# Attention in a hybrid diffusion block: a pair's products with the values split over two rounds, and the scaled maximum moved from ScalarE to GpSimd

## The chip, the cores and the metric

One Trainium2 chip, and of it one core. The metric is the device time of one execution of the whole program in microseconds (us), a median over runs. TensorE (PE, with its weight loads shown as PEld), VectorE (DVE), ScalarE (ACT), GpSimd (POOL) and SyncE (SP) each run their own instruction stream in order, and meet only at semaphores.

## What is computed

A two-layer backbone over 512 latent and 256 context tokens of width 1024. Layer 0 mixes tokens with grouped-query attention, layer 1 with a long convolution; both are followed by an MLP. The change touches only the attention of layer 0, for the latent queries:

```python
def gqa_attend(q, k, v):
    s = jnp.einsum('bqkgd,bskd->bkgqs', q, k).astype(jnp.float32) * (q.shape[-1] ** -0.5)
    p = jax.nn.softmax(s, axis=-1).astype(v.dtype)
    return jnp.einsum('bkgqs,bskd->bqkgd', p, v)
```

There are 8 query heads of width 128 over 2 key/value heads, 512 queries and 768 keys. The queries and keys are RMS-normed before; the kernel leaves the query's root out of the scores and applies it as the factor `rq`, one number per query row and tile.

## The kernel before

The work is written by hand, one stream per engine, with a semaphore for each kind of result. A value in full precision is held as two rounded parts, hi and lo, and a product is three matmuls (`mm3`: hi by hi, hi by lo, lo by hi).

The attention runs in rounds n. There are NQ = 32 tiles of scores, one for each head and each group of 128 queries; a tile is 128 queries by 768 keys and fills a bank pair in PSUM. What the engines do for tile m is spread over the rounds:

- round m: TensorE makes the scores of tile m (six matmuls), VectorE takes each row's negated maximum (`nmax`, L1383).
- round m+1: ScalarE scales it by `rq` into `bmax` (L870) and makes the exponentials with `bmax` as bias, with their row sums beside (L871, signalled by `exp_done`).
- round m+2: VectorE inverts the row sum (L1371) and scales the row in place (L1372, `p_done`).
- round m+3: TensorE turns the tile by six transposes (L1878, `pt_done`), ScalarE copies it out of PSUM as `phi` (L861), VectorE makes `plo` (L1377).
- a pair of tiles then goes through the products with the values: 18 matmuls of 256 columns in `prob_values`, whose result ScalarE copies to `hhi` (L854) and VectorE completes as `hlo` (`o_lo`, L1356).

There are three bank pairs, used in turn by scores and turned tiles: `score(n)` is the pair 2n+1 and `turned(m)` the pair 2(m+3), each modulo 3. So the transposes in round n write the bank pair from which the exponential of round n-1 read, and TensorE waits for it:

```python
pe.wait_ge(p_done, m + 1)
pe.wait_ge(exp_done, min(n - 1, NQ))
```

Within a round each engine's order is fixed by the code: TensorE transposes tile n-3, makes the scores of tile n, and in odd rounds from 5 on does the products of a pair. ScalarE makes `hhi` (even rounds from 6 on), `phi` of tile n-3, `bmax` and the exponential of tile n-1. VectorE scales tile n-2, makes `plo` of tile n-3 and `nmax` of tile n, then `hlo` (even rounds from 6 on), and in every fourth round (n % 4 == 3) a row of the modulation of layer 0, `ada_row`, one pass of 1024 elements over two operands in SBUF (L1362). GpSimd has no work in the attention. Its last work ahead of it is the DMAs of the rotary part, and the next after it is `load_tables`, which waits for the eighth `ada_row`.

Of the kernel before, what the change touches and what calls it, by code (L numbers as in the profile page):

```python
# [27 lines left out]
ALU = mybir.AluOpType  # L28
ACT = mybir.ActivationFunctionType
# [8 lines left out]
KT = NK // P  # L38
# [50 lines left out]
def build(nc, xT, ctxT, cT, cols, wpack, ahead, apack, fw1, fw2, fw3, featsT, decay, tables, consts, ropes, fdram, out):  # L89
    with ExitStack() as ctx:  # L90
# [3 lines left out]
        def sem(name):  # L94
            return ctx.enter_context(nc.semaphore(name))
# [25 lines left out]
        nmax = sb("nmax", [P, 2])  # L121
# [4 lines left out]
        rq = sb("rq", [P, NH * QT])  # L126
        bmax = sb("bmax", [P, 2])
# [92 lines left out]
        crow_done = sem("crow_done")  # L220
# [39 lines left out]
        rq_done = sem("rq_done")  # L260
# [10 lines left out]

        score_done = sem("score_done")
        nmax_done = sem("nmax_done")
        exp_done = sem("exp_done")
        rinv_done = sem("rinv_done")
        p_done = sem("p_done")
# [2 lines left out]
        plo_done = sem("plo_done")  # L279
        pv_done = sem("pv_done")  # L280
        ohi_done = sem("ohi_done")
        olo_done = sem("olo_done")
# [107 lines left out]
        NQ = NH * QT  # L390
# [186 lines left out]
        @block.gpsimd  # L577
        def _(pool):
            nc.gpsimd.memset(epst[:, :], EPS).then_inc(eps_set, 1)
            TTP = nc.gpsimd.tensor_tensor  # L580

            def filter_los(n):
                q, tt = divmod(n, 4)
                hi, lo = FPAIR[q % 2]
                pool.wait_ge(eo_hi, 2 * n + 1)
                TTP(lo[:, tt, :], FE[n % 2], f(hi[:, tt, :]), ALU.subtract).then_inc(eo_lo, 1)
                pool.wait_ge(eo_hi, 2 * n + 2)
                TTP(lo[:, 4 + tt, :], FO[n % 2], f(hi[:, 4 + tt, :]), ALU.subtract).then_inc(eo_lo, 1)

            def x_add(i):  # L590

                pool.wait_ge(xsq_done, i + 2)
                if i:
                    pool.wait_ge(xadd_done, i)
                TTP(XSQ[:, 0, :], XSQ[:, 0, :], XSQ[:, 1, :], ALU.add).then_inc(xadd_done, 1)

            for n in range(8):
                filter_los(n)
            pool.wait_ge(acol_done, 16)
            pool.dma_start(araw[:, :, 0:NT], ropes).then_inc(rope_in, 16)  # L600
            x_add(0)
            for n in range(8, 16):
                filter_los(n)
                if n in (8, 9):
                    x_add(n - 7)
                if n == 9:
                    pool.wait_ge(xadd_done, 3)
                    TTP(XSQ[:, 0, 0:NT], XSQ[:, 0, 0:NT], XSQ[:, 0, NT:2 * NT], ALU.add).then_inc(xadd_done, 1)
            for t in range(QKV_UNITS + 2):
                for n, (u, ps, w, r, key, hi, lo) in turned_jobs(t):  # L610
                    if r is None:
                        continue
                    if key:
                        pool.wait_ge(job_qn, key_of(n))
                    else:
                        pool.wait_ge(evac_done, u + 1)
                    if r >= 2:
                        pool.wait_ge(job_full, r - 1)
                    q = P // 4
                    for o in range(4):  # L620
                        i = o ^ 1
                        pool.dma_start(ROTATED[r % 2][o * q:(o + 1) * q, :],
                                       value_of(n)[i * q:(i + 1) * q, :]).then_inc(rot_in[r % 2], 16)

            def load_tables(third):

                if third:
                    pool.wait_ge(tlo_done, third + 1)
                else:
                    pool.wait_ge(arow_done, ADA_ATT)  # L630
                pool.dma_start(S[:, 8:10, :], tables[:, 2 * third:2 * third + 2, :]).then_inc(table2_in, 16)

            def y_sums(b):

                for j in range(1, KC - 1):
                    if b == 0 and j in (1, 2, 4):
                        load_tables(j // 2)
                    pool.wait_ge(ysq_done, KC * b + j + 1)
                    nc.gpsimd.tensor_tensor(S[:, 11, :], S[:, 11, :], S[:, 10, :], ALU.add).then_inc(yacc_done, 1)  # L639
                    pool.wait_ge(yacc_done, (KC - 2) * b + j)  # L640

            y_sums(0)
            y_sums(1)
            pool.wait_ge(arow_done, ADA_ROWS)

            def load_spectrum(m):
                o, c = STAGES[m // 2]
                if m:
                    pool.wait_ge(filt_used, m)
                else:  # L650
                    for n in range(2):
                        pool.wait_ge(filt_out[n], 8 * 16)
                pool.dma_start(araw[:, :, :].rearrange("p a (b n) -> p (a b) n", b=2),
                               fdram[2 * (2 * c + o) + m % 2]).then_inc(filt_in, 16)

            for m in range(8):
                load_spectrum(m)
            y_sums(2)
            y_sums(3)
# [3 lines left out]
        def _(act):  # L663
            own = Own(act, own_act)
            A = nc.scalar.activation
# [137 lines left out]
            for t in range(QKV_UNITS + 2):  # L803
# [20 lines left out]
                for i, (n, (_, ps, w, r, key, hi, lo)) in enumerate(jobs_of(t)):  # L824
# [6 lines left out]
                    if key:  # L831
                        ins = A(value_of(n), ps, ACT.Copy)
                    else:
# [3 lines left out]
                        ins = A(value_of(n), ps, ACT.Copy, scale=qg[:, 0:1])  # L837
# [9 lines left out]
                      AB[:, :, 0:3 * P].rearrange("p a (b c) -> p a b c", b=3), ACT.Copy).then_inc(vhi_done, 1)  # L847


            for n in range(NQ + 5):  # L850
                if n >= 6 and n % 2 == 0:
                    m = (n - 6) // 2
                    act.wait_ge(pv_done, m + 1)
                    A(hhi[:, m // 2, (m % 2) * 2 * P:(m % 2 + 1) * 2 * P], (B2, B3)[m % 2][:, 0:2 * P],  # L854
                      ACT.Copy).then_inc(ohi_done, 1)
                m = n - 3
                if 0 <= m < NQ:
                    act.wait_ge(pt_done, m + 1)
                    if m >= 4:
                        act.wait_ge(pv_done, m // 2 - 1)  # L860
                    A(phi[:, m // 2 % 2, :, (m % 2) * P:(m % 2 + 1) * P],  # L861
                      turned(m).rearrange("p (b c) -> p b c", b=KT), ACT.Copy).then_inc(phi_done, 1)
                m = n - 1
                if 0 <= m < NQ:
                    act.wait_ge(nmax_done, m + 1)
                    if m >= 2:
                        act.wait_ge(pt_done, m - 1)
                    if m == 0:
                        act.wait_ge(rq_done, 1)
                    own(A(bmax[:, m % 2:m % 2 + 1], nmax[:, m % 2:m % 2 + 1], ACT.Copy, scale=rq[:, m:m + 1]))  # L870
                    A(PROB[m % 2], score(m), ACT.Exp, bias=bmax[:, m % 2:m % 2 + 1], scale=rq[:, m:m + 1],  # L871
                      accum_out=rsum[:, m % 2:m % 2 + 1]).then_inc(exp_done, 1)
                if n == 1:
                    act.wait_ge(csum_done, 1)
                    A(crow[:, 0:NT], B2[:, :], ACT.Copy).then_inc(crow_done, 1)
                    A(crow[:, NT:2 * NT], B3[:, :], ACT.Copy).then_inc(crow_done, 1)
# [205 lines left out]
        def _(dve):  # L1082
# [270 lines left out]
            def o_lo(m):  # L1353
                dve.wait_ge(ohi_done, m + 1)
                cols_ = slice((m % 2) * 2 * P, (m % 2 + 1) * 2 * P)
                TT(hlo[:, m // 2, cols_], (B2, B3)[m % 2][:, 0:2 * P], f(hhi[:, m // 2, cols_]), ALU.subtract).then_inc(olo_done, 1)  # L1356
# [5 lines left out]
                nc.vector.tensor_tensor_reduce(slot, slot, crow if early else crow1[:, :], 1.0, 0.0, ALU.mult, ALU.add,  # L1362
                                               dst).then_inc(arow_done, 1)

            for n in range(NQ + 5):
                m = n - 2
                if 0 <= m < NQ:
                    dve.wait_ge(exp_done, m + 1)
# [10 lines left out]
                if n < NQ:  # L1379
                    dve.wait_ge(score_done, n + 1)  # L1380
                    if n >= 2:
                        dve.wait_ge(exp_done, n - 1)
                    nc.vector.tensor_reduce(out=nmax[:, n % 2:n % 2 + 1], in_=score(n), op=ALU.max,  # L1383
                                            axis=AX.X, negate=True).then_inc(nmax_done, 1)
                if n >= 6 and n % 2 == 0:
                    o_lo((n - 6) // 2)
                if n < NQ and n % 4 == 3:
                    r = n // 4
                    if r == 0:
# [304 lines left out]
        def _(pe):  # L1694
# [160 lines left out]
                                 start=True, stop=True)  # L1855
                    ins.then_inc(job_ss, 1)

            def prob_values(m):

                pe.wait_ge(plo_done, 2 * m + 2)  # L1860
                if m == 0:
                    pe.wait_ge(crow_done, 2)
                if m >= 2:
                    pe.wait_ge(olo_done, m - 1)
                g = m // 2 // GROUP
                for kt in range(KT):
                    ins = mm3((B2, B3)[m % 2][:, 0:2 * P], vhi[:, kt, g, :], vlo[:, kt, g, :],
                              phi[:, m % 2, kt, :], plo[:, m % 2, kt, :], kt == 0, kt == KT - 1)
                ins.then_inc(pv_done, 1)


            for n in range(NQ + 4):
                m = n - 3
                if 0 <= m < NQ:
                    pe.wait_ge(p_done, m + 1)
# [18 lines left out]
                if n == 1:  # L1894
                    pe.wait_ge(cdiag_done, KC)
                    mm(B2[:, :], ones, S[:, 4, :], start=True, stop=True)
                    mm(B3[:, :], ones, S[:, 5, :], start=True, stop=True).then_inc(csum_done, 1)
                if n >= 5 and n % 2 == 1:
                    prob_values((n - 5) // 2)

            def square_column(src, first, last):

# [267 lines left out]
```

## Time and profile before

| | |
|---|---|
| median of 3 runs | 1483.09 us (1483.0 to 1486.6) |
| the profiled execution | 1486.4 us, span of its instructions 1484.6 us |
| busy share of the span | PE 92%, PEld 76%, DVE 60%, ACT 42%, POOL 8% |
| mean granted TensorE clock | 0.969 |
| in the attention, 226 to 340 us | PE 90.76, DVE 92.55, ACT 73.95, POOL 0.56 us busy |

The profile is one execution. Busy time is time in which an instruction ran; an idle time is given with what ended it. For matmuls a row's length includes the pipeline, so that the distance between two starts says more than the length. Other engines too begin an instruction up to 0.1 us before the row of the one ahead has ended.

### The profile page before, as it was taken

The page shows a single profiled execution, that of the slowest core. Times are in us where ns is not written, and L with a number is a line of the kernel's source. Part 1 is how long each engine was busy: PE and PEld are TensorE (multiplying, and loading weights), DVE is VectorE, ACT ScalarE, POOL GpSimd, SP SyncE. Part 2 cuts the span into 40 slices and gives each one's busy share as a digit, 9 for nine tenths or more (in the row PEclk, how much of TensorE's full clock was granted, in tenths as well). Part 3 has the DMA queues.
Part 4 walks back from the last instruction along what each step waited for, and adds up shares of the span by engine and source line. Part 5 has one row for each costly group of instructions (what it writes and reads, how often), then busy time and mean ns, then how long its engine had stood idle before and what let it go on. Part 6 is the DMA issues. An engine that isn't in the chain of part 4 may idle for free. (4 is left out here: it accounts for less than half of the span.)

```text
span 1484.6 us, 17999 instructions
## 1 busy us (share of the span) xinstructions
PE 1369.2 (92%) x6614; PEld 1130.2 (76%) x6614; DVE 897.1 (60%) x1291; ACT 626.2 (42%) x950; POOL 113.9 (8%) x117
## 2 busy tenths in 40 slices
PE   7889997888899999999988999999889999999996
PEld 2467786777688888888878777888768888888885
DVE  7668767886765555555446799998446333333333
ACT  4445436664353242423435434243435334152441
POOL 1661120001100000000010000000110000000001
PEclk9999999999899999999989999999989999999998
DMA  9434240106536566565321212221312223223221
GB/s 368 168 125 175 88 164 29 43 15 218 193 94 219 183 197 200 184 202 180 113 99 42 85 60 100 75 82 58 102 54 72 102 98 99 99 86 105 92 85 57
DMA packets 49416, 178.47 MB, mean 120 GB/s; under 512 B 5991, under 2 KB 8359, under 8 KB 46920
## 3 DMA queue, kind: packets, MB, share of 16 engines
q1 hardware_dynamic: 46344, 164.51, 32.7%
q0 software_dynamic: 3008, 13.11, 2.8%
q8 instruction: 39, 0.64, 0.2%
q14 instruction: 25, 0.20, 0.0%
HBM read 164.49 MB, written 10.49 MB: 118 GB/s over the span
## 5 line engine op out<-in xcount | busy, mean ns | idle before, releaser
L1699 PE MATMUL bank<-hhi,whi 128*128 128x512 f32 (+1 forms) x936 | 352.6, 377 | 10.2 <-ACT scratch L955 5.6
L1701 PE MATMUL bank<-hhi,wlo 128*128 128x512 f32 (+1 forms) x936 | 349.8, 374 | 0.0
L1700 PE MATMUL bank<-hlo,whi 128*128 128x512 f32 (+1 forms) x936 | 349.5, 373 | 0.0
L1091 DVE TENSOR_TENSOR wlo<-raw,whi 128x1024 fp32r<-128x1024 f32 x180 | 223.2, 1241 | 96.9 <-ACT whi L672 95.7
L672 ACT ACTIVATE whi<-raw 128x1024 fp32r<-128x1024 f32 x180 | 189.5, 1053 | 216.2 <-PE bank L1701 199.4
L1699 PE MATMUL bank<-ghi,whi 128*128 128x512 f32 x576 | 225.0, 391 | 4.7 <-DVE glo L1624 2.8
L1700 PE MATMUL bank<-glo,whi 128*128 128x512 f32 x576 | 224.8, 390 | 0.0
L1701 PE MATMUL bank<-ghi,wlo 128*128 128x512 f32 x576 | 224.6, 390 | 0.0
L1699 PEld LDWEIGHTS bank<-hhi,whi 128*128 128x128 f32 x936 | 176.6, 189 | 42.2 <-ACT whi L672 9.9
L1701 PEld LDWEIGHTS bank<-hhi,wlo 128*128 128x128 f32 x936 | 176.6, 189 | 31.5
L1700 PEld LDWEIGHTS bank<-hlo,whi 128*128 128x128 f32 x936 | 176.8, 189 | 30.7
L1485 DVE TENSOR_TENSOR glo<-scratch,ghi 128x512 fp32r<-128x512 f32 x64 | 44.4, 693 | 180.2 <-ACT ghi L959 180.2
L1699 PEld LDWEIGHTS bank<-ghi,whi 128*128 128x128 f32 x576 | 108.4, 188 | 28.1 <-DVE glo L1624 3.2
L1701 PEld LDWEIGHTS bank<-ghi,wlo 128*128 128x128 f32 x576 | 108.5, 188 | 22.7
L1700 PEld LDWEIGHTS bank<-glo,whi 128*128 128x128 f32 x576 | 108.5, 188 | 22.4
L955 ACT ACTIVATE scratch<-bank 128x512 f32<-128x512 f32 x64 | 38.2, 597 | 159.7 <-PE bank L1701 159.7
L1497 DVE TENSOR_TENSOR scratch<-scratch,bank 128x512 f32<-128x512 f32 x48 | 33.0, 687 | 109.2 <-PE bank L1701 109.2
L639 POOL TENSOR_TENSOR scratch<-scratch 128x512 f32<-128x512 f32 x24 | 32.7, 1362 | 859.2 <-ACT scratch L886 859.2
L1699 PE MATMUL bank<-t2hi,ghi 128*128 128x256 f32 x128 | 38.4, 300 | 11.5 <-DVE glo L1597 11.5
L1878 PE MATMUL bank<-consts,scratch 128*128 128x128 f32 x192 | 27.3, 279 | 22.9 <-ACT scratch L871 22.9
L1935 PE MATMUL bank<-scratch,consts 128*128 128x256 f32 x96 | 32.8, 516 | 13.2 <-ACT scratch L918 13.2
L1362 DVE CUSTOM_DVE_ANT_0 araw<-araw,crow 128x1024 f32<-128x1024 f32 x36 | 43.6, 1218 | 0.0
(259 smaller groups left out, 2014.3 us busy)
## 6 DMA issues: line engine op xcount, KB each, us to landing
raw<-in_wpack SPq DMA_DIRECT2D x180, 512.0 KB, 3.4
araw<-in_apack SPq DMA_DIRECT2D x40, 512.0 KB, 3.4
amore<-in_apack SPq DMA_DIRECT2D x36, 512.0 KB, 3.5
ablk<-in_ahead SPq DMA_DIRECT2D x8, 1024.0 KB, 12.7
spectra<-scratch SPq DMA_DIRECT2D x16, 512.0 KB, 3.2
araw<-spectra POOLq DMA_DIRECT2D x8, 1024.0 KB, 5.0
fs<-in_fw SPq DMA_DIRECT2D x2, 1024.0 KB, 11.1
x<-in_xT SPq DMA_DIRECT2D x1, 2048.0 KB, 13.7
```

The costliest lines, as they stand in the source:

```text
L639: nc.gpsimd.tensor_tensor(S[:, 11, :], S[:, 11, :], S[:, 10, :], ALU.add).then_inc(yacc_done, 1)
L672: A(whi[:, s, :], raw[:, r, :], ACT.Copy).then_inc(hi_done, 1)
L955: A(S[:, 8 + j % 2, :], bank, ACT.Relu).then_inc(evac_done, 1)
L1091: TT(wlo[:, s, :], raw[:, r, :], f(whi[:, s, :]), ALU.subtract).then_inc(lo_done, 1)
L1362: nc.vector.tensor_tensor_reduce(slot, slot, crow if early else crow1[:, :], 1.0, 0.0, ALU.mult, ALU.add, dst).then_inc(arow_done, 1)
L1485: TT(glo[:, j, :], S[:, 10 + j % 2, :], f(ghi[:, j, :]), ALU.subtract).then_inc(g_done, 1)
L1497: TT(y[:, j, :], y[:, j, :], AB[:, j % 2, :], ALU.add).then_inc(evac_done, 1)
L1699: mm(o, lh, rh, start=first, stop=False)
L1700: mm(o, lh, rl, start=False, stop=False)
L1701: return mm(o, ll, rh, start=False, stop=last)
L1878: ins = nc.tensor.transpose(turned(m)[:, kt * P:(kt + 1) * P], PROB[m % 2][:, kt * P:(kt + 1) * P], ident)
L1935: ins = mm(XSUM[h], ones, y[:, j, at], start=j == 0, stop=j == KC - 1)
```

## The change

Three edits. `prob_values` takes a half: the first three of the six blocks of keys of a pair's products in one round, the other three in the next, behind that round's transposes and scores. The copies `hhi` and `o_lo` of a pair come one round later with it, so in odd rounds from 7 on, and the loops have one more round. The product of `nmax` and `rq` is made by a GpSimd loop of 32 one-column instructions, with a semaphore of its own (`bmax_done`), and ScalarE's instruction for it and its wait on itself are gone.

```diff
--- before.py
+++ after.py
@@ -271,6 +271,7 @@
 
         score_done = sem("score_done")
         nmax_done = sem("nmax_done")
+        bmax_done = sem("bmax_done")
         exp_done = sem("exp_done")
         rinv_done = sem("rinv_done")
         p_done = sem("p_done")
@@ -621,6 +622,15 @@
                         i = o ^ 1
                         pool.dma_start(ROTATED[r % 2][o * q:(o + 1) * q, :],
                                        value_of(n)[i * q:(i + 1) * q, :]).then_inc(rot_in[r % 2], 16)
+
+            for m in range(NQ):
+                pool.wait_ge(nmax_done, m + 1)
+                if m == 0:
+                    pool.wait_ge(rq_done, 1)
+                if m >= 2:
+                    pool.wait_ge(exp_done, m - 1)
+                nc.gpsimd.tensor_tensor(bmax[:, m % 2:m % 2 + 1], nmax[:, m % 2:m % 2 + 1], rq[:, m:m + 1],
+                                        ALU.mult).then_inc(bmax_done, 1)
 
             def load_tables(third):
 
@@ -847,9 +857,9 @@
                       AB[:, :, 0:3 * P].rearrange("p a (b c) -> p a b c", b=3), ACT.Copy).then_inc(vhi_done, 1)
 
 
-            for n in range(NQ + 5):
-                if n >= 6 and n % 2 == 0:
-                    m = (n - 6) // 2
+            for n in range(NQ + 6):
+                if n >= 7 and n % 2 == 1:
+                    m = (n - 7) // 2
                     act.wait_ge(pv_done, m + 1)
                     A(hhi[:, m // 2, (m % 2) * 2 * P:(m % 2 + 1) * 2 * P], (B2, B3)[m % 2][:, 0:2 * P],
                       ACT.Copy).then_inc(ohi_done, 1)
@@ -862,12 +872,9 @@
                       turned(m).rearrange("p (b c) -> p b c", b=KT), ACT.Copy).then_inc(phi_done, 1)
                 m = n - 1
                 if 0 <= m < NQ:
-                    act.wait_ge(nmax_done, m + 1)
+                    act.wait_ge(bmax_done, m + 1)
                     if m >= 2:
                         act.wait_ge(pt_done, m - 1)
-                    if m == 0:
-                        act.wait_ge(rq_done, 1)
-                    own(A(bmax[:, m % 2:m % 2 + 1], nmax[:, m % 2:m % 2 + 1], ACT.Copy, scale=rq[:, m:m + 1]))
                     A(PROB[m % 2], score(m), ACT.Exp, bias=bmax[:, m % 2:m % 2 + 1], scale=rq[:, m:m + 1],
                       accum_out=rsum[:, m % 2:m % 2 + 1]).then_inc(exp_done, 1)
                 if n == 1:
@@ -1362,7 +1369,7 @@
                 nc.vector.tensor_tensor_reduce(slot, slot, crow if early else crow1[:, :], 1.0, 0.0, ALU.mult, ALU.add,
                                                dst).then_inc(arow_done, 1)
 
-            for n in range(NQ + 5):
+            for n in range(NQ + 6):
                 m = n - 2
                 if 0 <= m < NQ:
                     dve.wait_ge(exp_done, m + 1)
@@ -1382,8 +1389,8 @@
                         dve.wait_ge(exp_done, n - 1)
                     nc.vector.tensor_reduce(out=nmax[:, n % 2:n % 2 + 1], in_=score(n), op=ALU.max,
                                             axis=AX.X, negate=True).then_inc(nmax_done, 1)
-                if n >= 6 and n % 2 == 0:
-                    o_lo((n - 6) // 2)
+                if n >= 7 and n % 2 == 1:
+                    o_lo((n - 7) // 2)
                 if n < NQ and n % 4 == 3:
                     r = n // 4
                     if r == 0:
@@ -1855,21 +1862,23 @@
                                  start=True, stop=True)
                     ins.then_inc(job_ss, 1)
 
-            def prob_values(m):
-
-                pe.wait_ge(plo_done, 2 * m + 2)
-                if m == 0:
-                    pe.wait_ge(crow_done, 2)
-                if m >= 2:
-                    pe.wait_ge(olo_done, m - 1)
+            def prob_values(m, half):
+
+                if half == 0:
+                    pe.wait_ge(plo_done, 2 * m + 2)
+                    if m == 0:
+                        pe.wait_ge(crow_done, 2)
+                    if m >= 2:
+                        pe.wait_ge(olo_done, m - 1)
                 g = m // 2 // GROUP
-                for kt in range(KT):
+                for kt in range(half * KT // 2, (half + 1) * KT // 2):
                     ins = mm3((B2, B3)[m % 2][:, 0:2 * P], vhi[:, kt, g, :], vlo[:, kt, g, :],
                               phi[:, m % 2, kt, :], plo[:, m % 2, kt, :], kt == 0, kt == KT - 1)
-                ins.then_inc(pv_done, 1)
-
-
-            for n in range(NQ + 4):
+                if half:
+                    ins.then_inc(pv_done, 1)
+
+
+            for n in range(NQ + 5):
                 m = n - 3
                 if 0 <= m < NQ:
                     pe.wait_ge(p_done, m + 1)
@@ -1895,8 +1904,8 @@
                     pe.wait_ge(cdiag_done, KC)
                     mm(B2[:, :], ones, S[:, 4, :], start=True, stop=True)
                     mm(B3[:, :], ones, S[:, 5, :], start=True, stop=True).then_inc(csum_done, 1)
-                if n >= 5 and n % 2 == 1:
-                    prob_values((n - 5) // 2)
+                if n >= 5:
+                    prob_values((n - 5) // 2, (n - 5) % 2)
 
             def square_column(src, first, last):
```

On ScalarE, in rounds 6 to 8 of the attention, these are the instructions before (`scratch,rsum<-bank,bmax,rq` is the exponential):

```order
L854 ACTIVATE hhi<-bank 128x256 [waits pv_done]
L861 ACTIVATE phi<-bank 128x6x128 [waits pt_done]
L870 ACTIVATE bmax<-nmax,rq 128x1 [waits pt_done,nmax_done]
L871 ACTIVATE scratch,rsum<-bank,bmax,rq 128x768 [waits own_act]
L861 ACTIVATE phi<-bank 128x6x128 [waits pv_done,pt_done]
L870 ACTIVATE bmax<-nmax,rq 128x1 [waits pt_done,nmax_done]
L871 ACTIVATE scratch,rsum<-bank,bmax,rq 128x768 [waits own_act]
L854 ACTIVATE hhi<-bank 128x256 [waits pv_done]
L861 ACTIVATE phi<-bank 128x6x128 [waits pv_done,pt_done]
L870 ACTIVATE bmax<-nmax,rq 128x1 [waits pt_done,nmax_done]
L871 ACTIVATE scratch,rsum<-bank,bmax,rq 128x768 [waits own_act]
```

and after the change (its lines stand up to 10 lower in the code):

```order
L871 ACTIVATE phi<-bank 128x6x128 [waits pt_done]
L878 ACTIVATE scratch,rsum<-bank,bmax,rq 128x768 [waits pt_done,bmax_done]
L864 ACTIVATE hhi<-bank 128x256 [waits pv_done]
L871 ACTIVATE phi<-bank 128x6x128 [waits pv_done,pt_done]
L878 ACTIVATE scratch,rsum<-bank,bmax,rq 128x768 [waits pt_done,bmax_done]
L871 ACTIVATE phi<-bank 128x6x128 [waits pv_done,pt_done]
L878 ACTIVATE scratch,rsum<-bank,bmax,rq 128x768 [waits pt_done,bmax_done]
```

The copy to `bmax` is gone from each round, the exponential waits for `bmax_done` in its place, and `hhi` has moved from rounds 6 and 8 to round 7.

On VectorE, rounds 6 and 7 before (`ISA` is the row of the modulation with its read-out):

```order
L1371 RECIPROCAL rinv<-rsum 128x1 [waits p_done,exp_done]
L1372 TENSOR_SCALAR scratch<-scratch,rinv 128x768 [waits own_dve]
L1377 TENSOR_TENSOR plo<-bank,phi 128x6x128 [waits phi_done]
L1383 TENSOR_REDUCE nmax<-bank 128x1 [waits exp_done,score_done]
L1356 TENSOR_TENSOR hlo<-bank,hhi 128x256 [waits ohi_done]
L1371 RECIPROCAL rinv<-rsum 128x1 [waits p_done,exp_done]
L1372 TENSOR_SCALAR scratch<-scratch,rinv 128x768 [waits own_dve]
L1377 TENSOR_TENSOR plo<-bank,phi 128x6x128 [waits phi_done]
L1383 TENSOR_REDUCE nmax<-bank 128x1 [waits exp_done,score_done]
L1362 ISA araw,mods<-araw,scratch 128x1024 [waits arow_in1]
L1362 ISA mods 128x1
```

and after:

```order
L1378 RECIPROCAL rinv<-rsum 128x1 [waits p_done,exp_done]
L1379 TENSOR_SCALAR scratch<-scratch,rinv 128x768 [waits own_dve]
L1384 TENSOR_TENSOR plo<-bank,phi 128x6x128 [waits phi_done]
L1390 TENSOR_REDUCE nmax<-bank 128x1 [waits exp_done,score_done]
L1378 RECIPROCAL rinv<-rsum 128x1 [waits p_done,exp_done]
L1379 TENSOR_SCALAR scratch<-scratch,rinv 128x768 [waits own_dve]
L1384 TENSOR_TENSOR plo<-bank,phi 128x6x128 [waits phi_done]
L1390 TENSOR_REDUCE nmax<-bank 128x1 [waits exp_done,score_done]
L1363 TENSOR_TENSOR hlo<-bank,hhi 128x256 [waits ohi_done]
L1369 ISA araw,mods<-araw,scratch 128x1024 [waits arow_in1]
L1369 ISA mods 128x1
```

`hlo` has left round 6 and stands in round 7, ahead of the modulation row; the number of instructions is the same.

## Rows read from the trace of the kernel before

**Rows 1.** Windows view: length, busy PE, PEld, DVE, ACT, POOL, granted clock, DMA, GB/s.
```profile
226.00:340.00 114.00, 90.76 (x645) 82.59 (x643) 92.55 (x156) 73.95 (x146) 0.56 (x1) 0.99 0.10 33
```

**Rows 2.** Waits from 226 to 345 us: engine, line, releaser, total, times, longest.
```profile
PE bank L1878 <- ACT scratch L871: 22.9, 17, 2.8
ACT phi L861 <- PE bank L1878: 22.1, 32, 1.6
...
DVE plo L1377 <- ACT phi L861: 18.3, 31, 1.9
```

**Rows 3.** Timeline of TensorE, rounds 15 to 17: start, length, instruction, idle before.
```profile
272.94 0.85 PE L1878 MATMUL bank<-consts,scratch 128*128 128x128 f32 x6 [1.23 <-ACT scratch L871]
...
274.68 0.29 PE L1699 MATMUL bank<-phi,vhi 128*128 128x256 f32 x1
...
276.84 0.82 PE L1878 MATMUL bank<-consts,scratch 128*128 128x128 f32 x6
...
279.95 0.84 PE L1878 MATMUL bank<-consts,scratch 128*128 128x128 f32 x6 [1.23 <-ACT scratch L871]
```

**Rows 4.** Timeline of ScalarE: an early exponential, rounds 15 and 16, and the last exponential.
```profile
243.69 0.99 ACT L871 ACTIVATE scratch<-bank,bmax,rq 128x768 f32<-128x768 f32 x1
...
273.82 0.82 ACT L861 ACTIVATE phi<-bank 128x768 fp32r<-128x768 f32 x1 [1.03 <-PE bank L1878]
274.53 0.28 ACT L870 ACTIVATE bmax<-nmax,rq 128x1 f32<-128x1 f32 x1
274.85 0.99 ACT L871 ACTIVATE scratch<-bank,bmax,rq 128x768 f32<-128x768 f32 x1
...
277.69 0.81 ACT L861 ACTIVATE phi<-bank 128x768 fp32r<-128x768 f32 x1 [0.27 <-PE bank L1878]
...
278.72 0.99 ACT L871 ACTIVATE scratch<-bank,bmax,rq 128x768 f32<-128x768 f32 x1
...
334.77 0.99 ACT L871 ACTIVATE scratch<-bank,bmax,rq 128x768 f32<-128x768 f32 x1
```

**Rows 5.** Timeline of VectorE: a stretch without a wait, and one `hlo`.
```profile
234.48 1.21 DVE L1362 CUSTOM_DVE_ANT_0 araw<-araw,scratch 128x1024 f32<-128x1024 f32 x1
...
235.62 0.16 DVE L1371 RECIPROCAL rinv<-rsum 128x1 f32<-128x1 f32 x1
235.81 0.62 DVE L1372 TENSOR_SCALAR scratch<-scratch,rinv 128x768 f32<-128x768 f32 x1
236.50 0.96 DVE L1377 TENSOR_TENSOR plo<-bank,phi 128x768 fp32r<-128x768 f32 x1
237.37 0.95 DVE L1383 TENSOR_REDUCE nmax<-bank 128x1 f32<-128x768 f32 x1
238.24 0.15 DVE L1371 RECIPROCAL rinv<-rsum 128x1 f32<-128x1 f32 x1
...
245.25 0.42 DVE L1356 TENSOR_TENSOR hlo<-bank,hhi 128x256 fp32r<-128x256 f32 x1
245.58 0.15 DVE L1371 RECIPROCAL rinv<-rsum 128x1 f32<-128x1 f32 x1
```

**Rows 6.** GpSimd's own instruction on 512 elements, length min/median/max.
```profile
L639 POOL TENSOR_TENSOR scratch<-scratch x24: 1287/1295/1942, 356.9 to 1462.7; 128x512 f32<-128x512 f32 x24
```

**Rows 7.** Timelines of VectorE, GpSimd and ScalarE where the first two meet.
```profile
42.03 4.02 DVE L1256 TENSOR_TENSOR tlo<-scratch,thi 128x3072 fp32r<-128x3072 f32 x1 [1.55 <-ACT thi L749]
...
42.79 4.39 POOL L588 TENSOR_TENSOR hlo<-fs,hhi 128x512 fp32r<-128x512 f32 x1
...
66.25 3.62 DVE L1091 TENSOR_TENSOR wlo<-raw,whi 128x1024 fp32r<-128x1024 f32 x1 [0.22 <-ACT whi L672]
...
66.36 2.41 POOL L595 TENSOR_TENSOR ablk<-ablk 128x1024 f32<-128x1024 f32 x1
...
68.81 1.06 ACT L727 ACTIVATE ablk<-x 128x1024 f32<-128x1024 f32 x1 [2.59 <-POOL ablk L595]
```

**Rows 8.** All instructions of VectorE's L1091, length min/median/max.
```profile
L1091 DVE TENSOR_TENSOR wlo<-raw,whi x180: 1214/1225/3615, 66.2 to 1448.0; 128x1024 fp32r<-128x1024 f32 x180
```

## The prediction

> **What bounds the kernel now.** I read the windows by stage first: over the attention no engine is full. TensorE is busy for 90.76 of 114 us, VectorE for 92.55, ScalarE for 73.95, at a granted clock of 0.99 [rows 1]. So the stage is held by a chain that goes round between engines, and the waits view names it: TensorE waits for the exponential 17 times, 22.9 us in all, ScalarE for the transposes (22.1), VectorE for `phi` (18.3) [rows 2].
>
> The timelines give the chain, start to start. Rounds go in pairs of 7.01 us, from the transposes at 272.94 to those at 279.95, in two unequal parts [rows 3]:
>
> - The round with products, 3.90 us: transposes and scores 1.74 (272.94 to 274.68), products 2.16 (274.68 to 276.84). TensorE doesn't pause; meanwhile ScalarE waits.
> - The round without, 3.11 us: transposes to `phi` 0.85, `phi` to the exponential 1.03 (0.71 to `bmax`, 0.32 for it), the exponential to the next transposes 1.23, for which TensorE waited [rows 3, 4].
>
> The bound changes sides every round: TensorE for one, ScalarE's loop for the other. From the exponential at 243.69 to that at 334.77 there are 26 rounds in 91.08 us, 3.50 each [rows 4].
>
> **The change part by part.** *Products in halves.* Each round from 5 on holds 1.74 + 1.08 = 2.82 us of TensorE. The sum of the work is the same, but no round has 3.90 any more.
>
> *`bmax` off ScalarE.* The loop of transposes, `phi`, exponential, transposes loses 0.32: 0.85 + 0.71 + 1.23 = 2.79.
>
> *What is late next.* VectorE. Its steps without a wait, start to start, are: reciprocal 0.19, scaling 0.69, `plo` 0.87, `nmax` 0.87, together 2.62; an `hlo` adds 0.33 every second round and the modulation row 1.14 every fourth [rows 5]. Four rounds hold 4 x 2.62 + 2 x 0.33 + 1.14 = 12.28, that is 3.07 each. VectorE is above 2.82 and 2.79, so it becomes the bound. `hlo` and the modulation row now share a round (4.09 us), against 2.95 and 3.76 apart before; as VectorE is then late all the time, only the sum counts. The time of GpSimd's result decides whether the others can keep up with it.
>
> *GpSimd's step.* The trace has no GpSimd instruction of one column. 512 elements take 1.295 us [rows 6] and 1024 take 2.41 [rows 7]; the line through both leaves 2 x 1.295 - 2.41 = 0.18 for none, so I take 0.2 as an estimate. From above it is bounded by the 1.3 of the 512-element row. A handoff from GpSimd took 0.04 us (the ScalarE row at 68.81, behind an end at 68.77) [rows 7]; for that from VectorE I assume 0.15. Before, the scaled maximum took ScalarE 0.32; now it is there about 0.39 after the end of `nmax`. This is hidden where it is ready before `phi` ends: from the start of `plo` to the end of `nmax` 0.87 + 0.95 pass, and the exponential is due one round after, so that about 1 us is free.
>
> *The shared way to SBUF.* A VectorE subtraction of 1024 elements with both operands in SBUF usually takes 1.225 us [rows 8]. The one at 66.25 took 3.62 and ended 1.1 us after the GpSimd instruction at 66.36 had ended; at 42.79 a 512-element GpSimd instruction took 4.39 us and ended 1.13 after the VectorE instruction over which it lay [rows 7]. So the two exclude each other, for a whole instruction. The Trainium skill (GPSIMD Engine Reference, Key points) says that GpSimd contends with VectorE instructions that have two SBUF inputs, where the trace agrees, or that run in a 2-port mode. By that the scaling of the row (L1372) is held too, and no row here shows it; its 768 elements in 0.62 us against 0.95 for `nmax` [rows 5] say only that it is the fast kind.
>
> I price both. Without exclusion there: 3.07 a round. With it: the scaling starts 0.87 + 0.19 = 1.06 after `nmax` starts, just ahead of GpSimd's turn at 0.95 + 0.15 = 1.10, so GpSimd waits to 1.68 and the exponential can start at 1.92. Behind it come 1.23 to the transposes, 0.85 to `phi`, 0.85 to `plo` (0.81 and a handoff), 0.87 to `nmax`: 5.72 for two rounds, where VectorE's own order needs 2.62 + 0.33 + 2.62 = 5.57. That is 0.15 late. In the next two rounds `phi` comes 0.19 late for the same reason and GpSimd's 0.1 stands ahead of the modulation row. So 0.44 in four rounds: 12.72, or 3.18 each. I take this one, as the rows that exist show exclusion.
>
> *Start and end.* In the rounds before the first products only the 0.32 goes, in about three of them: 0.9. At the end the transposes of the last tile stand behind half of the products of the pair before, not all, so that its `plo` and the last products come 1.1 earlier (2.16 - 1.08). The added round has no work of its own. GpSimd's loop is done before the eighth modulation row, for which `load_tables` behind it waits anyway; the modulation rows' DMAs move with the rounds. What follows the attention starts earlier by as much and keeps its length.
>
> **The sum.** 26 x (3.50 - 3.18) = 8.3, with 0.9 and 1.1: 10.3 us. Without exclusion 26 x 0.43 = 11.2 and 2.0: 13.2. The profiled execution took 1486.4 us (span 1484.6 and 1.8 around it), so 1476.1; it lies 3.3 above the median of the runs. From the median of 1483.1 it is 1472.8, or 1469.9 without exclusion.
>
> **Rivals.**
>
> - *The gap closes wholly* (20%): no exclusion on the scaling, 1470. For it: only instructions with two SBUF inputs are seen to exclude. Against it: the skill's rule, and GpSimd's turn falls right there.
> - *GpSimd is slower than the line through two sizes says* (17%): an instruction of 0.4 to 0.7 us. With exclusion it stands in VectorE's way in each pair and behind VectorE's scaling in the other round, some 0.5 us per round and us of it: 3.28 to 3.43 a round, which leaves 2 to 6 us of the 8 and 2 around it: 1475.5 to 1479.5. For it: GpSimd's lengths scatter (up to 1.942 for the same instruction [rows 6]), and it has a wait of its own for each.
> - *Slower than before* (5%): the same with about 0.9 us or more. By the rate above 3.18 + 0.5 x 0.7 = 3.53 is the 3.50 of before. At the 1.3 us of the 512-element row it would be 3.7, or 26 x 0.2 = 5 less 2 at the ends: 1486. Against it: one column is 1/512 of that row's work. The skill (GPSIMD Engine Reference, Engine selection) would have elementwise work on VectorE; here VectorE's round is the longest, and its rule has no price for one column.
> - *Nothing comes of the halves* (8%): something that I don't see holds the pair at about 7 us, such as a wait for `hlo` or a bank. The order of banks speaks against it: `hlo` of a pair is due two rounds before its accumulator is used again. Then only ScalarE's 0.32 in every second round is left, 13 x 0.32 = 4: 1479.
>
> **How the numbers follow.** My case, exclusion with a short GpSimd instruction, has 50%: 1471 to 1474.5. With the cases beside it the range is 1467.5 to 1480, which leaves out the slower case and part of the long GpSimd instructions. About 0.3% (4.4 us) is what a measurement of this kernel can tell from no change: faster than 1478.7 is 84%, within 11%, slower 5%.
>
> **What would show it.** In the changed kernel's profile the starts of transposes should stand some 2.8 to 3.9 apart, 12.7 in four rounds, with no half at 3.90 followed by 3.11. TensorE's wait for ScalarE should be small, VectorE's wait for `phi` fall from 18.3 to under 4 us, and GpSimd show 32 rows of about 0.2 us, half of them starting where a scaling ends. VectorE should be busy for nearly all of the rounds. The prediction is wrong if GpSimd's rows are over 0.4 us, if TensorE or ScalarE waits for `bmax`, or if the scaling is stretched well over 0.62.

## The result, and the profile after

The changed kernel takes 1463.59 us (median of 5 runs, 1462.61 to 1466.13), the one before 1483.09 (5 runs beside them, 1481.95 to 1486.6). The ratio is 0.9867, with a 95% interval of 0.9848 to 0.9885: 19.5 us faster, where 10.3 were forecast, and 4 us under the low end of the range. The direction was right and the mechanism partly; the size was wrong.

The profiled execution has a span of 1464.4 us, 20.2 less than before. First, where it lies. The copy behind the attention's last `hlo` (to `crow1`) starts at 344.88 us before and here at:

```profile
327.75 1.06 ACT L887 ACTIVATE crow<-scratch 128x1024 f32<-128x1024 f32 x1 [0.49 <-DVE hlo L1363]
```

So 17.1 us are won up to the end of the attention, and 3.1 behind it, where no line of the program was changed. The 17.1 divide into 14.5 in the 26 rounds between the exponentials of tiles 5 and 31 (76.59 us in place of the 91.08 of [rows 4], 2.95 a round in place of 3.50), 2.0 before them and 0.6 behind them.

The waits view from 226 to 335 us (engine, line, releaser, us, times, longest) answers to [rows 2]:

```profile
ACT phi L871 <- PE bank L1887: 24.7, 32, 1.2
...
ACT scratch L878 <- POOL bmax L632: 4.5, 8, 2.7
PEld bank L1887 <- DVE scratch L1379: 4.1, 8, 1.4
...
PE bank L1887 <- ACT scratch L878: 3.4, 3, 1.3
...
DVE plo L1384 <- ACT phi L871: 2.4, 5, 1.0
```

TensorE waits for the exponential 3.4 us where it waited 22.9, VectorE for `phi` 2.4 where it waited 18.3. The weight loads ahead of the transposes now wait for VectorE's scaling (4.1 us in eight times). ScalarE still waits for the transposes, which costs nothing: it is the engine with time to spare.

TensorE's transposes, four rounds, answer to [rows 3]:

```profile
248.71 0.87 PE L1887 MATMUL bank<-consts,scratch 128*128 128x128 f32 x6
...
251.92 0.85 PE L1887 MATMUL bank<-consts,scratch 128*128 128x128 f32 x6
...
254.74 0.84 PE L1887 MATMUL bank<-consts,scratch 128*128 128x128 f32 x6
...
257.55 0.83 PE L1887 MATMUL bank<-consts,scratch 128*128 128x128 f32 x6
...
260.54 0.87 PE L1887 MATMUL bank<-consts,scratch 128*128 128x128 f32 x6
```

The alternation of 3.90 and 3.11 is gone. Distances are 3.21, 2.82, 2.81 and 2.99, together 11.83 us for four rounds; the pattern repeats every four rounds, as the modulation row does. VectorE over the same four rounds, to be read beside [rows 5]:

```profile
247.84 0.16 DVE L1378 RECIPROCAL rinv<-rsum 128x1 f32<-128x1 f32 x1
248.04 0.62 DVE L1379 TENSOR_SCALAR scratch<-scratch,rinv 128x768 f32<-128x768 f32 x1
248.57 0.95 DVE L1384 TENSOR_TENSOR plo<-bank,phi 128x768 fp32r<-128x768 f32 x1
249.44 0.95 DVE L1390 TENSOR_REDUCE nmax<-bank 128x1 f32<-128x768 f32 x1
250.30 0.16 DVE L1378 RECIPROCAL rinv<-rsum 128x1 f32<-128x1 f32 x1
250.50 0.62 DVE L1379 TENSOR_SCALAR scratch<-scratch,rinv 128x768 f32<-128x768 f32 x1
...
255.74 0.62 DVE L1379 TENSOR_SCALAR scratch<-scratch,rinv 128x768 f32<-128x768 f32 x1
256.46 0.96 DVE L1384 TENSOR_TENSOR plo<-bank,phi 128x768 fp32r<-128x768 f32 x1
...
258.53 1.21 DVE L1369 CUSTOM_DVE_ANT_0 scratch<-scratch 128x1024 f32<-128x1024 f32 x1
...
259.67 0.16 DVE L1378 RECIPROCAL rinv<-rsum 128x1 f32<-128x1 f32 x1
```

From one reciprocal behind a modulation row to the next are 11.83 us. From the scaling at 248.04 to `plo` at 248.57 are 0.53 us, not the 0.69 that I took; only one such step in the four rounds is longer, 0.72 us up to the `plo` at 256.46. So VectorE works nearly without a pause, as forecast, but with shorter steps. GpSimd:

```profile
234.92 1.10 POOL L632 TENSOR_TENSOR bmax<-nmax,rq 128x1 f32<-128x1 f32 x1 [3.55 <-DVE nmax L1390]
...
250.47 0.19 POOL L632 TENSOR_TENSOR bmax<-nmax,rq 128x1 f32<-128x1 f32 x1 [3.75 <-DVE nmax L1390]
```

The instruction takes 0.19 us (0.2 was estimated). It starts 0.08 us after `nmax` has ended (249.44 + 0.95 = 250.39), where I had assumed 0.15, and so 0.03 us ahead of the scaling at 250.50. That scaling lasts 0.62 us and is followed by `plo` after 0.53, as elsewhere, though GpSimd's row lies over its first 0.16 us. The GpSimd instruction at 234.92 came behind the start of a modulation row and took until its end.

### The profile page after: what moved, and what is told of

Same layout as the page of the kernel before. It is cut to its first block and busy times, and to the rows that moved or that the text cites. A ratio compares the mean times of both kernels' runs of the same rounds, so it can differ in the third digit from the quotient of the medians.

```text
span 1464.4 us, 18029 instructions
## 1 busy us (share of the span) xinstructions
PE 1368.5 (93%) x6614; PEld 1127.9 (77%) x6614; DVE 894.8 (61%) x1291; ACT 618.0 (42%) x918; POOL 120.8 (8%) x149
## 5 line engine op out<-in xcount | busy, mean ns | idle before, releaser
L1706 PE MATMUL bank<-hhi,whi 128*128 128x512 f32 (+1 forms) x936 | 351.8, 376 | 10.3 <-ACT scratch L962 5.6
L1369 DVE CUSTOM_DVE_ANT_0 amore<-amore,crow 128x1024 f32<-128x1024 f32 x36 | 43.5, 1217 | 0.0
```

Of the source, the lines that this page charges most:

```text
L1706: mm(o, lh, rh, start=first, stop=False)
```

## The experiments

The first two rows are the runs of the result. The experiments were run beside the kernel before, in two groups of four, all on one chip. "26 rounds" is the time between the starts of the exponentials of tiles 5 and 31 in each one's profile.

| kernel | median us | before, beside it | ratio (95%) | 26 rounds, us | a round |
|---|---|---|---|---|---|
| before | 1483.09 | | | 91.08 | 3.50 |
| changed | 1463.59 | 1483.09 | 0.9867 (0.9848 to 0.9885) | 76.59 | 2.95 |
| halves only | 1470.55 | 1485.79 | 0.9911 (0.9886 to 0.9935) | 81.53 | 3.14 |
| GpSimd only | 1479.97 | 1485.79 | 0.9968 (0.9949 to 0.9988) | 86.93 | 3.34 |
| one more GpSimd instruction | 1469.25 | 1485.79 | 0.9896 (0.9879 to 0.9914) | 79.72 | 3.07 |
| no modulation rows | 1458.36 | 1485.79 | 0.9815 (0.9799 to 0.9832) | 73.07 | 2.81 |
| five more | 1474.35 | 1485.53 | 0.9925 (0.9898 to 0.9952) | 86.19 | 3.32 |
| `hlo` on GpSimd | 1459.98 | 1485.53 | 0.9831 (0.9804 to 0.9858) | 75.67 | 2.91 |
| and the row moved | 1462.54 | 1485.53 | 0.9842 (0.9819 to 0.9864) | 74.59 | 2.87 |
| changed, again | 1464.20 | 1485.53 | 0.9853 (0.9831 to 0.9876) | 76.58 | 2.95 |

**Each edit alone.** Halves only: the GpSimd loop is taken out of the changed kernel, and ScalarE has its instruction back.

```diff
-                    act.wait_ge(bmax_done, m + 1)
+                    act.wait_ge(nmax_done, m + 1)
...
+                    own(A(bmax[:, m % 2:m % 2 + 1], nmax[:, m % 2:m % 2 + 1], ACT.Copy, scale=rq[:, m:m + 1]))
```

> The changed kernel with the scaled maximum back on ScalarE; the products stay in halves. Theory (three loops, the longest sets the round: TensorE 2.82, ScalarE's loop 2.79 and 0.32 for the scaled maximum, VectorE 2.91 over four rounds): ScalarE's loop is then the bound at 3.11 in every round, so the attention gets 26 x (3.11 - 2.95) = 4.2 and some 0.5 us longer than in the changed kernel: about 1468, still 15 under the kernel before. Rival A (GpSimd's part brings nothing, all comes from the halves): 1463.6. Rival B (the halves bring nothing without it): close to 1483.

GpSimd only: the same difference the other way round, put into the kernel before.

> The kernel before with the scaled maximum on GpSimd; the products stay whole in odd rounds. Theory: a pair is 3.90 of TensorE and 2.79 of ScalarE's loop, 6.69 in place of 7.01, so 3.34 a round: 26 x 0.16 = 4.2 and about 1 us at the start under the kernel before, about 1478. If the two edits' gains add up, it and the halves alone give the whole; by the theory they would here almost add up (0.16 + 0.39 = 0.55 a round against 0.55 measured). Rival (what counts is ScalarE's relief): 1467 or so.

Transposes of the first, and then of the second:

```profile
259.10 0.85 PE L1880 MATMUL bank<-consts,scratch 128*128 128x128 f32 x6 [0.16 <-ACT scratch L871]
262.23 0.85 PE L1880 MATMUL bank<-consts,scratch 128*128 128x128 f32 x6 [0.15 <-ACT scratch L871]
```

```profile
261.49 0.82 PE L1885 MATMUL bank<-consts,scratch 128*128 128x128 f32 x6
264.27 0.85 PE L1885 MATMUL bank<-consts,scratch 128*128 128x128 f32 x6 [0.91 <-ACT scratch L878]
268.18 0.82 PE L1885 MATMUL bank<-consts,scratch 128*128 128x128 f32 x6
```

With the halves alone every round is 3.13 or 3.14, ScalarE's loop with its 0.32. With GpSimd alone rounds of 2.78 and 3.91 alternate, its loop without the 0.32 and TensorE's long round. The three loops of the theory give both, and the rivals fall. Of the 14.5 us in the rounds 9.6 come with the halves alone and 4.2 with GpSimd alone. The whole programs are 15.2 and 5.8 us shorter than the kernel before beside them; about 15 and 5 were forecast.

**Do the scaling and GpSimd exclude each other?** One more instruction ahead of each scaled maximum, into a free tile:

```diff
+                for j in range(1):
+                    nc.gpsimd.tensor_tensor(tap2[:, 0, 1 * m + j:1 * m + j + 1], nmax[:, m % 2:m % 2 + 1], rq[:, m:m + 1], ALU.mult)
```

> The changed kernel with one more GpSimd instruction of one column ahead of each scaled maximum, so that the second of them starts inside VectorE's scaling of the row (L1372 before). Work added, nothing left out. Theory 1 (that scaling and GpSimd don't exclude each other): both GpSimd rows last 0.19, the scaling stays 0.62, and the time grows by 0 to 2 us, 1463.6 to 1466. Theory 2 (they do, and in the changed kernel GpSimd just got in first by 0.03 us): the second GpSimd row lasts until the scaling ends, some 0.7 us, or the scaling is stretched, and a round gets 0.1 or more longer: 1467 to 1470.

GpSimd, and VectorE's scaling at the same moment:

```profile
248.13 0.19 POOL L633 TENSOR_TENSOR tap<-nmax,rq 128x1 f32<-128x1 f32 x1 [3.62 <-DVE nmax L1392]
248.28 0.55 POOL L634 TENSOR_TENSOR bmax<-nmax,rq 128x1 f32<-128x1 f32 x1
250.59 0.19 POOL L633 TENSOR_TENSOR tap<-nmax,rq 128x1 f32<-128x1 f32 x1 [1.76 <-DVE nmax L1392]
250.73 0.19 POOL L634 TENSOR_TENSOR bmax<-nmax,rq 128x1 f32<-128x1 f32 x1
```

```profile
248.16 0.62 DVE L1381 TENSOR_SCALAR scratch<-scratch,rinv 128x768 f32<-128x768 f32 x1
...
250.43 0.41 DVE L1365 TENSOR_TENSOR hlo<-bank,hhi 128x256 fp32r<-128x256 f32 x1
```

The second GpSimd instruction starts 0.12 us into the scaling and ends at 248.83, 0.05 after it; beside `hlo`, which reads one operand from PSUM, the pair of instructions isn't held (250.59 and 250.73). So the scaling holds a GpSimd instruction that comes after it. The Trainium skill (GPSIMD Engine Reference, Key points) has contention with VectorE instructions in a 2-port mode; the trace agrees if this scaling runs in one, which no row states. Theory 2 holds: in the changed kernel GpSimd escapes this by 0.03 us. With a turn 0.15 us later its result comes 0.51 us later where the scaling stands in the way, and that costs 0.12 a round, 3.1 us over the 26.

**Is VectorE the bound?** Its modulation rows are left out of the attention (eight columns of the modulation are then not computed):

```diff
-                    ada_row(r % ADA_RING, r // ADA_RING + 1, mods[:, 16 + r:17 + r], True)
+                    dve.wait_ge(arow_in[r % ADA_RING], 16 * (r // ADA_RING + 1))
+                    nc.vector.tensor_copy(mods[:, 16 + r:17 + r], arow_slot(r % ADA_RING, True)[:, 0:1]).then_inc(arow_done, 1)
```

> The changed kernel without the eight passes of 1024 elements of the modulation rows in the attention: a copy of one column stands in for each, so eight columns of the modulation are not computed. Theory (VectorE is the bound of the changed kernel): its four rounds fall from 11.64 to about 10.7, TensorE's 2.82 and ScalarE's 2.79 take over and a round is 2.82: 26 x (2.95 - 2.82) = 3.4 us and something at the ends, about 1459.5. Rival (another chain already holds the round at 2.95, VectorE is merely busy beside it): 1463.6.

All distances are now 2.81:

```profile
260.50 0.84 PE L1888 MATMUL bank<-consts,scratch 128*128 128x128 f32 x6
263.31 0.83 PE L1888 MATMUL bank<-consts,scratch 128*128 128x128 f32 x6
266.12 0.84 PE L1888 MATMUL bank<-consts,scratch 128*128 128x128 f32 x6
```

3.5 us go from the rounds, as expected, and then the round is at the 2.81 of TensorE, with ScalarE's loop close to it. VectorE was the bound.

**How late may the scaled maximum be?** The loop of the experiment with one more instruction, with 5 in place of 1.

> The changed kernel with five more one-column GpSimd instructions ahead of each scaled maximum, 0.15 us apart by the run with one more, so that the result comes 0.75 us later and more where VectorE's scaling stands in between. Theory (the two-round chain through GpSimd becomes the bound; nmax to exponential 0.95 + 0.08 + 0.75 + 0.19 + 0.04, plus 0.4 behind the scaling, then 1.23 + 0.85 + 0.85 + 0.87 = 6.2 for two rounds, and more beside a modulation row): 3.12 to 3.35 a round, the attention 4.5 to 10 us longer than in the changed kernel, still shorter than before. Rival (the slack of 1 us behind nmax hides it): 2.95 to 3.0 a round.

```profile
264.28 1.12 POOL L633 TENSOR_TENSOR tap<-nmax,rq 128x1 f32<-128x1 f32 x5 [1.76 <-DVE nmax L1392]
265.36 0.18 POOL L634 TENSOR_TENSOR bmax<-nmax,rq 128x1 f32<-128x1 f32 x1
```

Here the result comes 265.54 - 264.28 = 1.26 us after the turn, in place of 0.19. In one round of four the turn lies ahead of a modulation row, and the row and the scaling behind it both hold GpSimd:

```profile
260.33 1.74 POOL L633 TENSOR_TENSOR tap<-nmax,rq 128x1 f32<-128x1 f32 x5 [1.82 <-DVE nmax L1392]
262.02 0.50 POOL L634 TENSOR_TENSOR bmax<-nmax,rq 128x1 f32<-128x1 f32 x1
```

There it comes 2.19 us after the turn. A round takes 3.32, 0.37 more than in the changed kernel. So the slack is used up, with results 1.0 to 1.1 us later in three rounds and 2.0 in the fourth, and the kernel is still faster than before. How late it would have to be to use up the whole gain of 0.55 a round wasn't tried.

**A shorter VectorE.** For all pairs but the last, ScalarE copies the bank in full behind the exponential and GpSimd makes `hlo` from the copy:

```diff
+            def pool_o_lo(m):
+                pool.wait_ge(ofull_done, m + 1)
+                cols_ = slice((m % 2) * 2 * P, (m % 2 + 1) * 2 * P)
+                TTP(hlo[:, m // 2, cols_], tap2[:, m % 2, 0:2 * P], f(hhi[:, m // 2, cols_]), ALU.subtract).then_inc(olo_done, 1)
...
+                    A(tap2[:, m % 2, 0:2 * P], (B2, B3)[m % 2][:, 0:2 * P], ACT.Copy).then_inc(ofull_done, 1)
```

> The changed kernel with hlo of all pairs but the last made by GpSimd, from a full copy that ScalarE makes behind the exponential in place of the bank. VectorE's four rounds fall from 11.64 to 10.98, that is 2.75, under TensorE's 2.82. Theory 1 (busy sums): 2.82 a round, 26 x 0.13 = 3.4 us under the changed kernel. Theory 2 (the modulation row now starts at once behind nmax and GpSimd's scaled maximum waits for its end, 1.1 us): 2.90 to 2.94 a round, 0 to 1.3 us.

In the second version the modulation row also stands behind the scaling:

```diff
-                if n < NQ and n % 4 == 3:
-                    r = n // 4
+                if n >= 4 and n % 4 == 0 and n <= NQ:
+                    r = n // 4 - 1
```

> As the run before, and the modulation row stands behind the scaling of the next round in place of behind nmax, so that GpSimd comes to its turn ahead of it. By theory 2 of that run the round gets shorter than there, 2.82 to 2.91; by theory 1 nothing changes.

GpSimd in the first of them, where the modulation row starts at 266.79 and ends at 268.01:

```profile
266.96 1.10 POOL L638 TENSOR_TENSOR bmax<-nmax,rq 128x1 f32<-128x1 f32 x1 [1.56 <-DVE nmax L1405]
```

Theory 2: the scaled maximum is caught behind the row, and a round is 2.91. With the row moved it isn't, and a round is 2.87. In the rounds alone these versions win 0.9 and 2.0 us over the changed kernel. Their times, 1459.98 and 1462.54 against 1464.20 beside them, don't rank them. In the profiles the first is 2.6 us ahead of the second at the exponential of tile 5 (238.88 and 241.51), before the rounds that are compared. 1.0 us of this is there already at 219 us; the rest arises from 220 to 230 us, where the first had a granted clock of 1.00 and the second of 0.69 and 0.62.

> The changed kernel once more beside these, for its time on the same chip and for what in its time changes from one execution to the next: rounds of 2.95, and a start and a rest that differ by up to 3 us with the moments at which TensorE's clock is lowered and raised.

The rounds repeat to 0.01 us (76.59 and 76.58).

## Why the prediction was wrong

*What bounds the kernel before: right.* The two unequal rounds, 3.90 of TensorE and 3.11 of ScalarE's loop, are what the edits alone take apart one by one.

*Products in halves, and `bmax` off ScalarE: right.* 2.82 and 2.79 were forecast for the two loops; without VectorE's rows 2.81 are measured.

*What is late next: right in kind, wrong in size.* VectorE is the bound. The step of the prediction that failed here is its 0.69 from scaling to `plo`, taken as a step without a wait. In the kernel before `phi` was just being finished there:

```profile
235.65 0.82 ACT L861 ACTIVATE phi<-bank 128x768 fp32r<-128x768 f32 x1 [1.64 <-PE bank L1878]
```

It ends at 236.47, and `plo` started at 236.50 [rows 5]. The row bears no wait, since it lasted less than a tenth. The trace before had the step without a wait as well, where `nmax` and not `plo` follows the scaling:

```profile
228.82 0.62 DVE L1372 TENSOR_SCALAR scratch<-scratch,rinv 128x768 f32<-128x768 f32 x1
229.36 0.95 DVE L1383 TENSOR_REDUCE nmax<-bank 128x1 f32<-128x768 f32 x1
```

With 0.53 for it, VectorE's four rounds are 12.28 - 4 x 0.16 = 11.64. This is the larger part of the error, 0.16 a round or 4.2 us.

*GpSimd's step: the duration right (0.19), the handoff not.* I assumed 0.15 from VectorE and it is 0.08. By these 0.07 us the turn falls ahead of the scaling, and of the 32 rows none starts where a scaling ends, where half were forecast to.

*The shared way to SBUF: the mechanism right, its place not.* That the scaling excludes GpSimd is shown by the run with one more instruction. That it would do so in this kernel is the second step that failed: 0.44 in four rounds, 2.9 us. The run with one more instruction is near that case, and its four rounds are 4 x 3.07 = 12.3, where the forecast's 12.72 less the 0.64 of the first step gives 12.08. What stays in the changed kernel is smaller: 11.83 measured less 11.64. In the waits view ScalarE waits for GpSimd eight times, by its timeline mostly 0.26 us in the round behind a modulation row:

```profile
250.69 0.99 ACT L878 ACTIVATE scratch<-bank,bmax,rq 128x768 f32<-128x768 f32 x1 [0.26 <-POOL bmax L632]
...
252.80 0.82 ACT L871 ACTIVATE phi<-bank 128x768 fp32r<-128x768 f32 x1 [1.03 <-PE bank L1887]
253.51 0.99 ACT L878 ACTIVATE scratch<-bank,bmax,rq 128x768 f32<-128x768 f32 x1
...
255.61 0.81 ACT L871 ACTIVATE phi<-bank 128x768 fp32r<-128x768 f32 x1 [0.29 <-PE bank L1887]
```

From there to the late `plo` the rows join without a gap: the exponentials at 250.69 and 253.51 are each followed after 1.23 us by transposes (251.92 and 254.74), these by `phi`, and `plo` starts at 256.46, 0.04 after `phi` has ended. VectorE's own order would have had it at 255.74 + 0.53 = 256.27. The 0.19 between is the whole rest by these rows; no run takes this chain out.

*The sum.* 12.72 - 0.64 - 0.44 + 0.19 = 11.83 for four rounds. For the 26 rounds 14.5 us in place of 8.3.

*Start and end.* 2.0 and 0.6 in place of 0.9 and 1.1. At the exponential of tile 2 the two kernels are level (232.92 and 232.89). From that of tile 4 to that of tile 5 are 3.88 us before and 2.81 after, at a granted clock of 1.00 in both: the first pair's products already stand ahead of it, and the forecast for the start had only the 0.32 there. The rest mixes the edit with the clock: between 225 and 230 us TensorE was granted 0.98 before and 0.62 in the changed kernel, between 230 and 235 us 0.70 and 1.00. What each is worth there stays open, as does why the end brought 0.6.

*"What follows keeps its length": wrong for these two executions.* It took 1139.7 and 1136.6 us. Followed instruction by instruction, the lead stays at 17.0 to 17.2 us up to the first MLP and then grows in jumps: to 18.6 there, to 19.9 by 782 us, to 20.3 at the end. At the first, windows of the same work before (430 to 440) and after (413 to 423) differ in the granted clock, the column behind PEld, DVE, ACT and POOL:

```profile
430.00:435.00 5.00, 2.94 (x10) 2.36 (x11) 4.48 (x6) 4.91 (x8) 0.00 (x0) 0.84 0.29 80
435.00:440.00 5.00, 5.00 (x20) 4.04 (x19) 3.12 (x6) 0.97 (x2) 0.00 (x0) 0.82 0.99 266
```

```profile
413.00:418.00 5.00, 2.96 (x13) 2.48 (x14) 4.51 (x6) 4.91 (x8) 0.00 (x0) 1.00 0.31 95
418.00:423.00 5.00, 5.00 (x24) 4.14 (x23) 4.32 (x7) 3.68 (x6) 0.00 (x0) 1.00 0.95 314
```

Two executions of the changed kernel differ in the same way. The second had 0.67 granted from 415 to 420 us where the first had 1.00, and fell 1.6 us behind it there; from 762 to 772 us it had 1.00 and the first 0.83, and by 797 us it was 0.3 ahead. The other kernels' profiles have 1133.9 to 1136.9 us for the stretch behind the attention. So some 3 us of the 20.2 between these two profiles are of a size and at a place where executions of one program differ too; how much of the 19.5 between the medians is of this kind isn't settled.

The range missed because all of its cases were built on the same 0.69. Its low end took VectorE at 3.07, and no case let that term itself be wrong.

## What to carry to other kernels

When three engines pass work round, write down each one's loop, and expect an edit to bring down the round only to the next loop; here 3.50 is the mean of two, and 3.14, 3.34, 2.95 and 2.81 follow as loops are taken away. Hold each step that is taken as one without a wait against the end of what it waits for, for a short wait bears no label. The smallest distance isn't enough: 0.69 was the smallest of the 31 from scaling to `plo` before. What helps is the same instruction with another one behind it, or its length: on VectorE here the next one starts 0.07 to 0.09 us before a row has ended, which makes 0.53 or 0.54 of the scaling's 0.62. A tiny instruction on GpSimd was cheap here (0.19 us and 0.08 for the handoff) as long as it came to its turn before a VectorE instruction that excludes it. So it pays to put a VectorE instruction that reads PSUM, such as `hlo`, behind the one whose result GpSimd waits for, and not a long pass over two operands in SBUF.

## What the runs showed of the hardware

- A GpSimd instruction of one column takes 0.19 us on both operands in SBUF, 0.14 to 0.15 from start to start, and 1.10 us (234.92, 266.96) when it meets VectorE's pass of 1024 elements with two SBUF operands.
- VectorE's scaling of 768 elements from SBUF to SBUF (0.62 us) holds GpSimd to its end, 0.55 us in place of 0.19; `hlo` beside it, with an operand in PSUM, did not. A scaling that started 0.03 us after GpSimd's 0.19 us kept its 0.62.
- The lower clock level costs time at the start of the attention. From 220 to 235 us the run with one more instruction had 1.00 granted throughout, the changed kernel 0.70, 0.62 and 1.00 in stretches of 5 us. At 219 us the first was 1.07 us ahead (218.41 and 219.48), where both had 1.00, and at the exponential of tile 2 it was 2.74 ahead (230.15 and 232.89). So 1.7 us go with the clock; where the 1.07 comes from wasn't looked for.
- Single executions of one program differ by some us: the five of the changed kernel lie between 1462.61 and 1466.13.
